# A two-layer hybrid block on one core: the residual's reload, the norm rows' load and the order of the first slab's splits moved

## What is computed

```python
h = x
for i in range(2):
    u = rms_norm(h, mix_pre_g[i])
    m = mixer_ab(u, ...) if i == 0 else mixer_c(u, ...)
    h = h + rms_norm(m, mix_post_g[i])
    u = rms_norm(h, mlp_pre_g[i])
    h = h + rms_norm(square(relu(u @ w_up[i])) @ w_down[i], mlp_post_g[i])
    e = p[i] @ w_ple_proj[i]
    gate = sigmoid(h @ w_ple_gate[i])
    h = h + rms_norm(e * gate, ple_post_g[i])
```

## Time and profile before

| what | value |
|---|---|
| median of 3 runs | 2583.43 us (2582.63 to 2583.96) |
| profiled execution | 2586.88 us |
| its span | 2585.1 us |
| PE busy | 2512.6 us (97%) |
| DVE busy | 1431.1 us (55%) |
| ACT busy | 1089.7 us (42%) |
| POOL busy | 153.7 us (6%) |
| mean granted clock of PE | 0.991 |
| moved by DMA | 453.33 MB, mean 175 GB/s |

### The profile page before, as it was taken

One profiled execution on the slowest core, in us unless ns is written; L12 is line 12 of the kernel. 1 busy time (PEld: TensorE's weight loads), 2 busy tenths in 40 slices (PEclk: granted clock), 3 DMA queues, 4 the chain that ended last, 5 costly groups with the idle time before them and its releaser, 6 DMA issues.

```text
span 2585.1 us, 33509 instructions
## 1 busy us (share of the span) xinstructions
PE 2512.6 (97%) x14359; PEld 2078.1 (80%) x14359; DVE 1431.1 (55%) x1558; ACT 1089.7 (42%) x1202; POOL 153.7 (6%) x177
## 2 busy tenths in 40 slices
PE   7999989899999999999999999999999999999998
PEld 6888769777888888888877978787888888888876
DVE  5557764656544544545555667646544545545564
ACT  5445420455434334334444444645434334334442
POOL 4000334010000000000100000010000000000100
PEclk9999999899999999999999999999999999999999
DMA  7556512366565565565544655256566565565543
GB/s 251 182 180 216 171 31 82 103 194 207 188 194 181 195 194 181 194 193 181 195 163 128 193 179 163 92 190 210 180 195 193 181 195 186 188 195 180 194 165 129
DMA packets 224889, 453.33 MB, mean 175 GB/s; under 512 B 7897, under 2 KB 16407, under 8 KB 223467
## 3 DMA queue, kind: packets, MB, share of 16 engines
q1 hardware_dynamic: 219197, 430.63, 51.5%
q0 software_dynamic: 3648, 17.54, 2.1%
q10 hardware_dynamic: 1902, 3.07, 0.4%
HBM read 445.52 MB, written 2.10 MB: 173 GB/s over the span
## 4 chain that ended last, share of the span: by engine, by line
PE 92%; DVE 3%; ACT 2%; DMA 1%; issue 1%; SPq 0%; DVEq 0%; ACTq 0%
PE psum L293 27%; PE psum L295 27%; PE psum L294 27%; PE psum L783 1%; PE psum L898 1%; DMA raw<-in_w_mlp_up 1%; PE psum L1703 1%; PE psum L1684 1%; DVE wlo L282 1%; PE psum L1699 1%; DVE uTl L434 1%; PE psum L1038 0%; PE psum L1040 0%; PE psum L1039 0%; PE psum L412 0%
## 5 line engine op out<-in xcount | busy, mean ns | idle before, releaser
L282 DVE TENSOR_TENSOR wlo<-raw,whi 128x2048 fp32r<-128x2048 f32 (+1 forms) x408 | 937.9, 2305 | 755.5 <-ACT whi L277 755.2
L277 ACT ACTIVATE whi<-raw 128x2048 fp32r<-128x2048 f32 (+1 forms) x408 | 773.8, 1902 | 776.3 <-DMA raw<-in_w_mlp_down 332.0
L293 PE MATMUL psum<-whi,uTh 128*128 128x512 f32 (+2 forms) x2176 | 856.4, 394 | 23.2 <-DVE uTl L434 12.5
L295 PE MATMUL psum<-whi,uTl 128*128 128x512 f32 (+2 forms) x2176 | 844.7, 388 | 0.0
L294 PE MATMUL psum<-wlo,uTh 128*128 128x512 f32 (+2 forms) x2176 | 843.7, 388 | 0.0
L293 PEld LDWEIGHTS psum<-whi,uTh 128*128 128x128 f32 x2176 | 411.0, 189 | 113.0 <-issue 26.6
L295 PEld LDWEIGHTS psum<-whi,uTl 128*128 128x128 f32 x2176 | 410.5, 189 | 81.9
L294 PEld LDWEIGHTS psum<-wlo,uTh 128*128 128x128 f32 x2176 | 411.1, 189 | 80.6 <-issue 2.4
L293 PE MATMUL psum<-whi,hTh 128*128 128x512 f32 x1024 | 400.1, 391 | 0.0
L295 PE MATMUL psum<-whi,hTl 128*128 128x512 f32 x1024 | 398.6, 389 | 0.0
L294 PE MATMUL psum<-wlo,hTh 128*128 128x512 f32 x1024 | 398.4, 389 | 0.0
(11 more groups left out here) (371 smaller groups left out, 1476.0 us busy)
## 6 DMA issues: line engine op xcount, KB each, us to landing
raw<-in_w_mlp_up SPq DMA_DIRECT2D x128, 1024.0 KB, 5.5
raw<-in_w_mlp_down SPq DMA_DIRECT2D x128, 1024.0 KB, 5.1
raw<-in_ab_w_in SPq DMA_DIRECT2D x48, 1024.0 KB, 5.2
raw<-in_w_ple_gate SPq DMA_DIRECT2D x32, 1024.0 KB, 5.1
raw<-in_c_w_in SPq DMA_DIRECT2D x24, 1024.0 KB, 5.2
raw<-in_ab_w_out SPq DMA_DIRECT2D x16, 1024.0 KB, 5.2
raw<-in_c_w_out SPq DMA_DIRECT2D x16, 1024.0 KB, 5.1
raw<-in_c_w_in SPq DMA_DIRECT2D x12, 736.0 KB, 4.5
```

Of the source, the lines that this page charges most:

```text
L277: act.activation(whi[:, q, :, 0:n], raw[:, q, :, 0:n], ACT.Copy).then_inc(hi_ready, 1)
L282: dve.tensor_tensor(wlo[:, q, :, 0:n], raw[:, q, :, 0:n], whi[:, q, :, 0:n].bitcast(F32), ALU.subtract).then_inc(lo_ready, 1)
L293: pe.matmul(o, xh, hi, start=(q == 0 and k == 0), stop=False)
L295: last = pe.matmul(o, xl, hi, start=False, stop=(q == 3 and k == 3))
```

## The change

Four parts:

- The four gains' rows come by two DMAs of 32 rows instead of four of 16.
- In the first slab the copies of a transposed quarter stand ahead of the split of the weight chunk of the same number, on ACT and DVE. The squares of quarter b stand behind the split of chunk b + 1, those of the last two behind the fourth split. `prologue` serves the output matrix alone.
- POOL issues the loads of `lnx_g` and `lnx_b` at the head of `rwkv_pool`, behind a wait for the last chunk of the last input slab.
- SP issues quarter q of the residual behind chunk q of the second output slab, and no more between the two.

```diff
--- before.py
+++ after.py
@@ -382,18 +382,19 @@
 
     def act_first(act, st, s, n, gain, squares=None):
 
+        first = st == order[0]
         for b in range(4):
-            if st != order[0] and b == 0:
+            if not first and b == 0:
                 split_hi(act, s, 2, n)
             T_act(act, st, b, gain)
-            if b == 0 and st == order[0]:
-                split_hi(act, s, 1, n)
-            if squares:
-                squares(b)
-            if b >= 2 and st == order[0]:
+            if first:
                 split_hi(act, s, b, n)
-            if b == 1 and st != order[0]:
+            if squares and b:
+                squares(b - 1)
+            if not first and b == 1:
                 split_hi(act, s, 3, n)
+        if squares:
+            squares(3)
 
 
     GROUPS = ((0, 0), (0, 1), (1, 0), (1, 1), (0, 2), (1, 2), (0, 3), (1, 3))
@@ -659,10 +660,7 @@
 
     def x_first(dve, link, st, s, n, gain):
 
-        T_dve(dve, st, 0, gain)
-        split_lo(dve, s, 1, n)
-        T_dve(dve, st, 1, gain)
-        for b in (2, 3):
+        for b in range(4):
             T_dve(dve, st, b, gain)
             split_lo(dve, s, b, n)
         dve.wait_ge(*mark("h_sq", st, 8))
@@ -671,11 +669,8 @@
     def prologue(fn, eng, st):
 
 
-        if st == order[0]:
-            fn(eng, base[st], 0, width(st))
-        elif st.endswith("_out"):
-            for q in range(2):
-                fn(eng, base[st], q, width(st))
+        for q in range(2):
+            fn(eng, base[st], q, width(st))
 
     def free_of(st, i):
 
@@ -1165,7 +1160,6 @@
 
     def ab_in_act(act):
         st, b = "ab_in", base["ab_in"]
-        prologue(split_hi, act, st)
         act_first(act, st, b, W, GAIN[st], x_squares(act, st))
         for i, (dst, col, n) in enumerate(ab_slabs):
             s, hd = b + i, i - H0
@@ -1344,7 +1338,6 @@
 
     def ab_in_dve(dve, link):
         st, b = "ab_in", base["ab_in"]
-        prologue(split_lo, dve, st)
         x_first(dve, link, st, b, W, GAIN[st])
         for i, (_, _, n) in enumerate(ab_slabs):
             s, hd = b + i, i - H0
@@ -1619,14 +1612,15 @@
                     yield p, s_, h_
 
     def rwkv_pool(pool):
+        pool.wait_ge(mm_used, 4 * (base["ab_in"] + N_AB))
+        pool.dma_start(lnx_g[:], A["rwkv_lnx_g"][0].partition_broadcast(P)).then_inc(sem("lnx_in"), 16)
+        pool.dma_start(lnx_b[:], A["rwkv_lnx_b"][0].partition_broadcast(P)).then_inc(sem("lnx_in"), 16)
         pool.wait_ge(sem("rw_a"), 2)
         pool.wait_ge(sem("rw_gm"), 4)
         for tt in range(TT):
             pool.memset(Y1[tt][:], 0.0).then_inc(sem("level_set"), 1)
             pool.tensor_copy(Ti[tt][:], over16(c_id[:])).then_inc(sem("level_set"), 1)
             pool.tensor_copy(TTi[:, tt], over16(c_id[:])).then_inc(sem("level_set"), 1)
-        pool.dma_start(lnx_g[:], A["rwkv_lnx_g"][0].partition_broadcast(P)).then_inc(sem("lnx_in"), 16)
-        pool.dma_start(lnx_b[:], A["rwkv_lnx_b"][0].partition_broadcast(P)).then_inc(sem("lnx_in"), 16)
         tt_init_pool(pool, 0)
         pool.wait_ge(sem("rw_rk"), 2)
         pool.wait_ge(sem("ka_rk_in"), 32)
@@ -2446,9 +2440,9 @@
     @block.sync
     def _(sp):
 
-        for i, g in enumerate((A["mix_pre_g"][0], A["mix_pre_g"][1], A["mlp_pre_g"][0], A["mlp_pre_g"][1])):
-            sp.dma_start(g_rows[KT * i:KT * (i + 1), :], g.rearrange("(k p) -> k p", p=P)).then_inc(sem("gpre_in"), 16)
-
+        for i, n in enumerate(("mix_pre_g", "mlp_pre_g")):
+            sp.dma_start(g_rows[2 * KT * i:2 * KT * (i + 1), :], A[n].rearrange("l (k p) -> (l k) p", p=P))\
+                .then_inc(sem("gpre_in"), 16)
         for st in order:
             b = base[st]
             if st.startswith("mlp"):
@@ -2495,15 +2489,13 @@
                             sp.wait_ge(mm_used, 4 * (b + j) - 3 + q)
                             sp.dma_start(raw[:, q, :, :], w_chunks(mats[st], 0)[kc][:, :, jj * W:(jj + 1) * W])\
                                 .then_inc(landed[q], 16)
+                            if j == 1:
+                                c4 = slice(q * W, (q + 1) * W)
+                                sp.wait_ge(sem("dv1"), 14)
+                                sp.dma_start(h[:, :, c4], A["x"][0].rearrange("(t p) d -> p t d", p=P)[:, :, c4])\
+                                    .then_inc(sem("x_back"), 16)
                     else:
                         load_slab(sp, b + j, w_chunks(mats[st], 0), j * W, W)
-                    if st == "ab_out" and j == 0:
-
-                        sp.wait_ge(sem("dv1"), 14)
-                        for q in range(4):
-                            c4 = slice(q * W, (q + 1) * W)
-                            sp.dma_start(h[:, :, c4], A["x"][0].rearrange("(t p) d -> p t d", p=P)[:, :, c4])\
-                                .then_inc(sem("x_back"), 16)
         for tt in range(TT):
             for b in range(4):
 
@@ -2601,7 +2593,7 @@
     def _(pe):
 
         pe.wait_ge(sem("consts"), 1)
-        pe.wait_ge(sem("gpre_in"), 64)
+        pe.wait_ge(sem("gpre_in"), 32)
         pe.transpose(bank[7][:, 0:4 * KT], g_rows[:], ident[0:4 * KT, 0:4 * KT]).then_inc(sem("gpre_T"), 1)
         for st in order:
             if st.startswith("mlp"):
```

## The result

| | before | changed |
|---|---|---|
| median, beside the prediction's 2583.43 | 2582.63 us (5 runs, 2580.88 to 2583.96) | 2569.59 us (5 runs, 2565.24 to 2570.80) |
| ratio, 95% interval | | 0.9948 (0.9934 to 0.9963) |
| profiled execution, span | 2586.88, 2585.1 us | 2569.92, 2568.2 us |
| mean granted clock of PE | 0.991 | 0.994 |

The changed kernel is faster: 13.0 us between the medians, of which 11.5 were forecast. The time lies at the lowest edge of the range. The two profiled executions differ by 17.0 us. That is more than the medians do, and the experiments show most of the reason.

A forecast was written before the change was run, and what follows sets the result against it. PE was taken as the bound (92% of the chain), so only its stops and slow stretches could pay. First slab -3.5, norm rows 0, residual -8.0 sum to -11.5 us: 2571.9 from 2583.43, range 2569.5 to 2577.5.

The forecast's parts named there:

- the low clock: Recurrence, behind the 3.51 us stop: granted clock 0.51 for 13.5 us, forecast to go with the stop.
- Rival (a): Recurrence: the long stop is not the residual's and only the first slab pays, 2579.9 us; 7 in 100.
- Rival (b): Recurrence: the stop goes but the clock falls anyway, 2576.4 us; 12 in 100.
- Rival (c): First slab gives half or less, the residual all, about 2574.5 us; 7 in 100.
- Rival (d): Second and third output slabs: x's quarters hold up the weight chunks behind them, slower, 2589 us; 2 in 100.
- Two fewer bring all that lands in the first 20 us 0.9 us earlier.: Kernel start: two g_rows DMAs for four make SP's later loads land 0.9 us earlier.
- PE's start at 13.8: First slab: PE's first weight matmul at 13.8 us, 2.5 earlier, with transposes ahead of weight chunks.
- The second slab starts at 40.3 for 43.8: 3.5 us.: First slab's new order and fewer g_rows DMAs start the second slab 3.5 us earlier; bounds 2.6 and 4.1.
- Norm rows: 0.: POOL's earlier loads of the norm rows change nothing: 0, between a gain of 0.9 and a loss of 0.5.
- The stop of 3.51 us goes.: Recurrence, at 453.02: PE's stop, read as code delayed by 2 MB of x, goes when the residual moves.
- L2082 starts at 465.8 for 473.78: 8.0 us.: Recurrence: moving the residual brings the reduction L2082 8.0 us earlier; bounds 0, 3.5 and 10.6.
- The stop at 439.18 stays.: Recurrence: PE's 1.17 us stop lies in the first output slab's 4 MB, which aren't moved, so it stays.

The follow-up runs named there:

- e2_order_only: Kernel before with only the first slab's order changed, four g_rows DMAs kept: 2576.60 us, ratio 0.9987.
- e4_lnx_only: Kernel before with only POOL's loads of the two norm rows moved to the head of rwkv_pool: 2583.40 us, ratio 1.0005.
- e3_gains_only: Kernel before with only two g_rows DMAs for four: 2579.29 us, ratio 0.9994.
- f3_half_residual: Kernel before with residual quarters 2 and 3 moved behind the third and fourth chunk of the second output slab: 2578.83 us, ratio 0.9986.
- e6_pool_reload: Kernel before with the residual's four loads issued by POOL instead of SP, at their old place in time: 2576.62 us, ratio 0.9983.
- e1_residual_only: Kernel before with only the residual's reload moved behind the chunks of the second output slab: 2576.09 us, ratio 0.9976.
- f1_changed: The changed kernel as it is, measured once more: 2571.01 us, ratio 0.9958 against the kernel before.
- e8_burst: Changed kernel with all four residual quarters behind the first chunk of the second output slab: 2570.75 us, ratio 0.9960 against the kernel before.
- f5_changed_lnx_back: Changed kernel with the two norm rows' loads back at their old place: 2572.54 us, ratio 0.9958 against the kernel before.

## Why the prediction was right or wrong, point by point

*The sum and the rivals.* Forecast 2571.9, -11.5 us; measured -13.0 and, repeated, -10.8. The direction, the places and the late code held. What failed is a step of the largest term, that the low clock is a fixed part of the kernel before; it is taken up at the 8.0 us below. Rival (a) fell: PE's stop followed the transfer, 2.7 to 3.5 us with 2 MB, 1.87 with 1 MB, none with none. The Trainium skill (Runtime: NRT & Kernel Launch, Instruction fetch mechanics) gives PE room for 2048 instructions and calls the fetch mostly hidden; this trace does not agree in this stretch. Rival (b) fell: with the residual moved the clock behind L1791 was 1.00 in each profile. Rival (c), the first slab at half or less, is against the traces (4.3 us). Rival (d) fell in the burst.

*"Two fewer bring all that lands in the first 20 us 0.9 us earlier."* Right: 2.21 for 3.13 us at the issue, 0.9 at the landing; 0.8 of it reached the fourth chunk.

*PE's start at 13.8.* Right: 13.82.

*"The second slab starts at 40.3 for 43.8: 3.5 us."* The mechanism was right, the size too small: 39.5, 4.3 us. I shifted by the trace's own distance from PE's first matmul to group 2 on ACT, 8.34 us; it was 7.96. And the norm took 2.45 us where I had 2.75 with the reduce's gap. The squares were late as forecast (0.76 us of waiting on DVE), but not enough to stop PE, since the fourth chunk ended only at 39.46.

*Norm rows: 0.* Not contradicted: the part alone measured no gain, and the stop at 364 us stayed at 1.53 us without the load. In the changed kernel a gain of up to 2 us is neither shown nor excluded.

*"The stop of 3.51 us goes."* Right in each profile with the residual moved. The reading that code was late is borne out by the packets. Two of its supports were weaker than they looked: the 3 packets in the 22 us from 431 to 453 were all in before x was asked for at 447.62, and in the changed kernel the packets there are 3.5 to 5.5 us apart (445.5, 450.8, 454.2, 459.8) without a stop, where I had asked for 3 to 4.

*"L2082 starts at 465.8 for 473.78: 8.0 us."* This is the mis-sized term: alone it measured 6.2 us. The step that failed is "and the stop of 3.51 us goes, with the low clock behind it": it took one execution's low clock for a fixed part of the kernel. With the residual at its old place the long stop is in every profile, but the 13.5 us at the lower clock behind it are in two of four: the two long executions, 2586.88 and 2586.41 us, and not in `e2_order_only` (2574.98) and `e4_lnx_only` (2580.82). To see the term by itself, take the time to L2082 from the state update right ahead of the output weights' load. That leaves out what differed earlier. In the kernel before that update is the line here; in the changed kernel it starts at 421.71.

```profile
429.75 0.69 DVE L2065 TENSOR_TENSOR ST<-psum,WL 128x512 f32<-128x512 f32 x1 [0.20 <-PE psum L1760]
```

| the residual | profiles | from the update to L2082, us |
|---|---|---|
| old place, clock fell | before, `e3_gains_only` | 44.0, 44.1 |
| old place, clock held | `e4_lnx_only`, `e2_order_only` | 40.0, 38.5 |
| half of it there | `f3_half_residual` | 37.7 |
| old place, from POOL | `e6_pool_reload` | 36.4 |
| moved | `e1_residual_only`, changed, `f1_changed`, `e8_burst`, `f5_changed_lnx_back` | 35.7, 35.4, 36.8, 35.6, 35.9 |

Against 35.9, the mean of the last row, the residual cost 8.1 and 8.2 us where the clock fell, just what I forecast, and 4.1 and 2.6 where it held. The mean of the four is 5.8, beside 6.2 by the runs. (The short stops beside the output weights' load are in all these figures and vary by up to 2 us.) The kernel before lay between 2575.3 and 2586.7 us in 35 runs, the one with the residual moved between 2573.2 and 2577.3 in 11: the change takes away the long executions above all. I read the 3.4 us between profiled execution and median as a possible share of the profiler. More likely they were this: the profile had caught a long execution.

*The stop at 439.18 stays.* Right: 1.41 us in the changed kernel, with a second of 1.05 behind it, beside the same load.

*Why the sum still came out.* The first slab gave 0.8 us more than forecast, the residual 1.8 less in the mean. That leaves 10.5, inside both measurements' intervals. These are two errors of opposite sign, so that the sum came this near is partly luck.

## What to carry to other kernels

Here PE worked in many small instructions (358 matmuls in 14 us), and a large transfer that nobody waited for stopped it by holding up its code. Look for "issue" stops beside a load, and place the packets of the instruction queue around each of them: a wide gap whose last packet comes just ahead of PE's going on is the evidence, and a count over a wide window is not. Move such a load to a stretch of few, long instructions, not just to another time; half of the first output slab's load took its stop along when it was moved by 23 us, and lost it behind the last small product. And price what a stop brings behind it (a low clock) from several executions, since one profile shows only one of the outcomes.

## What the runs showed of the hardware that I had not expected

The same 2 MB stopped PE for 1.04 us from POOL's queue and for 2.7 to 3.5 us from SP's. Each of the long stops ended 2.3 to 2.6 us behind the landing of a code packet. Stops of 2.69 and 2.79 us were followed by a granted clock of 1.00 over the next 13 to 14 us (`e2_order_only`, `e4_lnx_only`), stops of 3.24 and 3.51 us by 0.50 to 0.51 (`e3_gains_only`, the kernel before). The length of the stop does not decide it by itself. Stops of 1.17, 1.25 and 1.46 us (the kernel before, `f3_half_residual`, `e2_order_only`) had the clock at 0.50 for at least 2 of the next 5 us, and one of 2.15 us (`e1_residual_only`) did not lower it. What does decide it is open.
